# Expert rows are added to the residual in memory by an accumulating scatter, and the norm behind the first expert stage moves into the next stage

## What is computed

```python
def rms_norm(x, g):
    return x * rsqrt(mean(x * x, axis=-1) + EPS) * g
...
    h = h + hier_moe(rms_norm(h, norm2_g), ...)      # 16 experts
    return rms_norm(h[:, N_META:], final_g)          # end of the first block
...
    u = rms_norm_2(h, norm_mix_g)                    # start of the second
...
    h = h + hier_moe_2(rms_norm_2(h, norm_ffn_g), ...)   # 32 experts; this is the output
```

## Time and profile before

| | us |
|---|---|
| median of 3 runs | 3065.0 |
| lowest and highest | 3061.52, 3066.18 |
| the profiled execution | 3058.05 |
| its span | 3056.3 |
| TensorE busy | 2683.7 (88%) |
| VectorE busy | 1508.0 (49%) |
| ScalarE busy | 1099.9 (36%) |
| GpSimd busy | 861.0 (28%) |

### The profile page before, as it was taken

The page is one execution under the profiler, slowest core; times in us unless marked ns, Lnnn a source line. Parts: engine busy times, 40 slices in busy tenths (PEclk is TensorE's granted clock), DMA queues, the critical chain, the costliest instruction groups (busy, mean ns, idle before and its releaser), DMA issues. The chain is left out here.

```text
span 3056.3 us, 33957 instructions
## 1 busy us (share of the span) xinstructions
PE 2683.7 (88%) x11990; PEld 1975.7 (65%) x11990; DVE 1508.0 (49%) x1832; ACT 1099.9 (36%) x1445; POOL 861.0 (28%) x748
## 2 busy tenths in 40 slices
PE   5999898999989699909999799898999989599994
PEld 3898555777768577706655455556777868577773
DVE  4295341222223588743266545443433543588885
ACT  3012332000012377741133344441331332377773
POOL 1232421212212154422100232322333322155441
PEclk9999899999999799958999899998999999799997
DMA  3110112112123599952422222322112113499998
GB/s 92 36 49 14 41 36 58 48 34 55 34 74 134 196 365 373 358 222 56 205 62 62 73 64 75 82 63 75 41 48 55 48 71 136 175 344 348 350 334 312
DMA packets 220932, 404.99 MB, mean 133 GB/s; under 512 B 41656, under 2 KB 160776, under 8 KB 198056
## 3 DMA queue, kind: packets, MB, share of 16 engines
q1 hardware_dynamic: 203560, 370.21, 35.8%
q0 software_dynamic: 17280, 33.59, 2.9%
HBM read 351.97 MB, written 76.68 MB: 140 GB/s over the span
## 5 line engine op out<-in xcount | busy, mean ns | idle before, releaser
L1920 DVE TENSOR_TENSOR moe_run_w_low_up<-moe_run_w,moe_run_w_high_up 128x2048 fp32r<-128x2048 f32 x116 | 265.4, 2289 | 103.4 <-ACT moe_run_w_high_up L1751 102.9
L1751 ACT CAST moe_run_w_high_up<-moe_run_w 128x2048 fp32r<-128x2048 f32 x116 | 221.3, 1908 | 103.1 <-DMA moe_run_w<-w_gate 54.0
L1697 PE MATMUL moe_run_up<-moe_run_w_high_up,moe_run_xT_high 128*128 128x512 f32 x464 | 193.4, 417 | 11.0 <-issue 10.9
L134 PE MATMUL rnn_ps<-uT_again_high,rnn_w_high 128*128 128x512 f32 x512 | 201.7, 394 | 0.0
L134 PE MATMUL rnn_ps<-uT_again_low,rnn_w_high 128*128 128x512 f32 x512 | 199.7, 390 | 0.0
L134 PE MATMUL rnn_ps<-uT_again_high,rnn_w_low 128*128 128x512 f32 x512 | 199.7, 390 | 0.0
L1697 PE MATMUL moe_run_up<-moe_run_w_low_up,moe_run_xT_high 128*128 128x512 f32 x464 | 184.0, 397 | 0.0
L1697 PE MATMUL moe_run_up<-moe_run_w_high_up,moe_run_xT_low 128*128 128x512 f32 x464 | 184.0, 397 | 0.0
L1225 DVE TENSOR_TENSOR merge_gated<-merge_branch,merge_gate 128x512 f32<-128x512 f32 x48 | 33.2, 691 | 302.1 <-ACT merge_gate L1210 302.1
L134 PE MATMUL merge_gates<-uT_high,merge_wg_high 128*128 128x512 f32 x384 | 170.2, 443 | 0.0
L1071 ACT ACTIVATE mla_probs<-mla_scores 128x512 f32<-128x512 f32 x192 | 94.2, 490 | 193.2 <-PE mla_scores L1003 138.6
(11 more groups left out here) (483 smaller groups left out, 6858.5 us busy)
## 6 DMA issues: line engine op xcount, KB each, us to landing
moe_run_w<-exp_w SPq DMA_DIRECT2D x72, 1024.0 KB, 9.0
moe_run_w<-w_gate SPq DMA_DIRECT2D x34, 1024.0 KB, 9.0
moe_run_w<-w_up SPq DMA_DIRECT2D x34, 1024.0 KB, 12.0
moe_run_w<-w_down SPq DMA_DIRECT2D x34, 1024.0 KB, 6.8
rnn_raw<-w_in SPq DMA_DIRECT2D x32, 512.0 KB, 3.9
merge_raw<-w_in SPq DMA_DIRECT2D x24, 512.0 KB, 3.8
norm_x<-x SPq DMA_DIRECT2D x16, 512.0 KB, 4.7
out_h<-x SPq DMA_DIRECT2D x16, 512.0 KB, 4.5
```

The source lines that it names most:

```text
L134: last = pe.matmul(out, a, b, start=(k == 0), stop=(k == n - 1))
L1697: last = pe.matmul(up[p][:], a, w, start=(h == 0 and k == 0), stop=(h == 1 and k == 3 * HK - 1))
L1751: act.copy(hi[p][j], raw[p][j][:]).then_inc(s_hi[j], 1)
L1920: dve.tensor_tensor(lo[p][j], raw[p][j][:], hi[p][j].bitcast(F32), ALU.subtract).then_inc(s_lo[j], 1)
```

## The change

In both expert stages the scatter goes to the residual itself (`h_d`, in the second stage the output) and adds the rows to what stands there. So ScalarE multiplies a result by a column of weights, `place_w`, as it copies it out of PSUM. That column holds the weight for each slot of each block; the stage's start computes it by one-hot products on TensorE, as the row numbers are. A scatter waits until the one before it has landed. One copy of two columns of `token` serves the scatter of block b and the gather of block b + 4, since both use token rows; it is made before the result is there. The table `y_d`, the loads of h and of `y_d`, the sums and the stores behind the loop are gone.

The norm with `final_g` moves into `norm3`: this stage loads the residual, makes the first norm in place, stores it to `x2` for later use, and makes its own norm of it into another tile, `z`. Each tile is squared, rooted and scaled twice.

```diff
-def norm_to_features(nc, cst, name, load, g_row, uT, first, prefetch):
+def norm_to_features(nc, cst, name, load, g_row, uT, first, prefetch, ahead=None):
...
+            def keep(sp, t):
+                sp.wait_ge(s_norm_a, t + 1)
+                sp.dma_start(ahead[1][t * P:(t + 1) * P, :], x[t % R][:]).then_inc(s_kept[t % R], 16)
...
+                    if t == 1 and ahead:
+                        sp.dma_start(ga[:], ahead[0].to_broadcast((P, D))).then_inc(s_ga, 16)
...
-                    if t >= R:
+                    if t >= R and ahead:
+                        keep(sp, t - R)
+                        sp.wait_ge(s_norm, t - R + 1)
+                        sp.wait_ge(s_kept[t % R], 16 * (t // R))
+                    elif t >= R:
                         sp.wait_ge(s_turn, 2 * (t - R) + 2)
...
+                if ahead:
+                    for t in range(n - R, n):
+                        keep(sp, t)
+                    for r in range(R):
+                        sp.wait_ge(s_kept[r], 16 * n // R)
...
+                def first_norm(t):
+                    act.wait_ge(s_x[t % R], 16 * (t // R) + 16)
+                    if t > 1:
+                        act.wait_ge(s_sum, t - 1)
+                    act.activation(junk[:], x[t % R][:], ACT.Square, accum_out=ss_a[:, t:t + 1]).then_inc(s_sum_a, 1)
+                    act.wait_ge(s_mean_a, t + 1)
+                    act.activation(root_a[:, t:t + 1], ms_a[:, t:t + 1], ACT.Sqrt).then_inc(s_root_a, 1)
+
+                def second_squares(t):
+                    act.wait_ge(s_norm_a, t + 1)
+                    act.wait_ge(s_sum_a, min(t + 2, n))
+                    act.activation(junk[:], x[t % R][:], ACT.Square, accum_out=ss[:, t:t + 1]).then_inc(s_sum, 1)
...
+                        if ahead:
+                            first_norm(t + 1)
...
+                        if ahead:
+                            second_squares(t)
...
+                def first_norm(t):
+                    at = slice(t, t + 1)
+                    dve.wait_ge(s_sum_a, t + 1)
+                    dve.tensor_scalar(ms_a[:, at], ss_a[:, at], 1.0 / D, EPS, ALU.mult, ALU.add).then_inc(s_mean_a, 1)
+                    dve.wait_ge(s_root_a, t + 1)
+                    dve.reciprocal(inv_a[:, at], root_a[:, at]).then_inc(s_inv_a, 1)
+                    if t == 0:
+                        dve.wait_ge(s_ga, 16)
+                    dve.wait_ge(s_inv_a, t + 1)
+                    dve.scalar_tensor_tensor(out=x[t % R][:], in0=x[t % R][:], scalar=inv_a[:, at], in1=ga[:],
+                                             op0=ALU.mult, op1=ALU.mult).then_inc(s_norm_a, 1)
...
-                        dve.scalar_tensor_tensor(out=x[t % R][0:rows, :], in0=x[t % R][0:rows, :],
+                        if ahead and t >= 2:
+                            dve.wait_ge(s_turn, 2 * (t - 2) + 2)
+                        dve.scalar_tensor_tensor(out=normed(t)[0:rows, :], in0=x[t % R][0:rows, :],
                                                  scalar=inv[0:rows, at], in1=g[0:rows, :], op0=ALU.mult,
                                                  op1=ALU.mult).then_inc(s_norm, 1)
...
-def run_experts(nc, cst, name, experts, logits, w1, w3, w2, v_d, y_d, h_d, g_row, out_d):
+def run_experts(nc, cst, name, experts, logits, w1, w3, w2, v_d, h_d):
...
-                if g_row is not None:
-                    sp.dma_start(g, g_row.to_broadcast((P, D))).then_inc(s_g, 16)
-                for t in range(NT):
-                    if t % 2 == 0:
-                        sp.wait_ge(s_lo[t // 2 % 2], 2 * n + 1 + t // 4)
-                    sp.dma_start(h[t], h_d[t * P:(t + 1) * P, :]).then_inc(s_h[t], 16)
                 for p in range(2):
                     sp.wait_ge(s_st[p], 16 * n + 16)
-                for t in range(NT):
-                    for k in range(2):
-                        at0 = k * S + t * P
-                        sp.dma_start(yk[t][k], y_d[at0:at0 + P, :]).then_inc(s_yk[t], 16)
-                for t in range(NT):
-                    if g_row is not None:
-                        sp.wait_ge(s_out, t + 1)
-                    else:
-                        sp.wait_ge(s_sum, t + 1)
-                    sp.dma_start(out_d[t * P:(t + 1) * P, :], h[t]).then_inc(s_kept, 16)
-                sp.wait_ge(s_kept, 16 * NT)
+                sp.sem_inc(s_go, 1)
...
-                def gather(b, p):
-                    pool.tensor_copy(idx[p][:], token[:, bass.ds(b, 1)]).then_inc(s_idx, 1)
-                    pool.wait_ge(s_idx, b - 1)
+                def gather(p):
                     pool.sem_inc(s_go, 1)
                     pool.indirect_dma_start(
                         out=x[p][:], out_offset=None, in_=v_d,
-                        in_offset=bass.IndirectOffsetOnAxis(ap=idx[p][:, 0:1], axis=0),
+                        in_offset=bass.IndirectOffsetOnAxis(ap=rows[p][:, 1:2], axis=0),
                         bounds_check=S - 1, oob_is_err=False).then_inc(s_x[p], 16)
 
-                def scatter(i, p):
-                    b = 2 * i + p
-                    pool.wait_ge(s_y, b + 1 + Y0)
-                    pool.sem_inc(s_go, 1)
-                    pool.tensor_copy(to[p][:], choice[:, bass.ds(b, 1)]).then_inc(s_to, 1)
-                    pool.wait_ge(s_to, b + 1)
+                def scatter(i, p, first=False):
+                    pool.wait_ge(s_y, 2 * i + p + 1 + Y0)
+                    if not (first and p == 0):
+                        pool.wait_ge(s_st[1 - p], 16 * i + 16 * p)
                     pool.sem_inc(s_go, 1)
                     pool.indirect_dma_start(
-                        out=y_d, out_offset=bass.IndirectOffsetOnAxis(ap=to[p][:, 0:1], axis=0),
+                        out=h_d, out_offset=bass.IndirectOffsetOnAxis(ap=rows[p][:, 0:1], axis=0),
                         in_=y[p][:], in_offset=None,
-                        bounds_check=2 * S - 1, oob_is_err=False).then_inc(s_st[p], 16)
+                        bounds_check=S - 1, oob_is_err=False, compute_op=ALU.add).then_inc(s_st[p], 16)
...
-                    gather(2 + p, p)
+                    pool.tensor_copy(rows[p][:, 1:2], token[:, 2 + p:3 + p]).then_inc(s_rows, 1)
+                    pool.wait_ge(s_rows, p + 1)
+                    gather(p)
                 pool.wait_ge(s_list, 1)
                 n = more(pool)
-                with pool.Fori(0, n) as i:
+
+                def one_pass(i, first=False):
                     for p in range(2):
-                        b = 2 * i + p + 4
-                        pool.wait_ge(s_turn, b - 1)
+                        b = 2 * i + p
+                        pool.wait_ge(s_turn, b + 3)
                         pool.sem_inc(s_go, 1)
-                        gather(b, p)
-                        scatter(i, p)
+                        pool.tensor_copy(rows[p][:], token[:, bass.ds(b, 2, 4)]).then_inc(s_rows, 1)
+                        pool.wait_ge(s_rows, b + 3)
+                        gather(p)
+                        scatter(i, p, first)
+
+                one_pass(0, True)
+                with pool.Fori(1, n) as i:
+                    one_pass(i)
                 for p in range(2):
+                    pool.tensor_copy(rows[p][:, 0:1], token[:, bass.ds(2 * n + p, 1)]).then_inc(s_rows, 1)
+                    pool.wait_ge(s_rows, 2 * n + p + 3)
                     scatter(n, p)
                 for p in range(2):
                     pool.wait_ge(s_x[p], 16 * n + 32)
                     pool.sem_inc(s_go, 1)
-                if g_row is not None:
-                    for t in range(NT):
-                        pool.wait_ge(s_h[t], 16)
-                        pool.wait_ge(s_weighted, t + 1)
-                        pool.tensor_tensor(h[t], h[t], y[t % 2][:], ALU.add).then_inc(s_first, 1)
...
+                def place_weights(k):
+                    pe.wait_ge(s_weighted, k + 1)
+                    for t in range(NT):
+                        last = pe.matmul(ps_w[:, 0:NB], in_block[k][:, t, :].bitcast(F32), weight_of[k][:, t, :],
+                                         start=(k == 0 and t == 0), stop=(k == 1 and t == NT - 1))
+                    last.then_inc(s_wsum, 1)
+
+                place_weights(0)
                 turn_rows(0, 0, True)
+                place_weights(1)
...
-                    act.copy(y[p][:], down[:]).then_inc(s_y, 1)
+                    act.mul(y[p][:], down[:], place_w[:, bass.ds(b, 1)]).then_inc(s_y, 1)
...
+                dve.wait_ge(s_exp, 2)
+                own(dve.tensor_reduce(tmp[:], gx[:], AX.X, ALU.add))
+                own(dve.reciprocal(gw[:], tmp[:]))
+                own(TS(tmp[:], ex[:], 1.0, None, ALU.add))
+                own(dve.reciprocal(tmp[:], tmp[:]))
+                own(TT(weights[:, 0, :], gw[:], tmp[:], ALU.mult))
+                own(TT(weights[:, 1, :], weights[:, 0, :], ex[:], ALU.mult))
...
-                own(TS(choice[:], ps_id[:, 0:NB], 2.0 * S, None, ALU.add))
...
```

(26 more changed lines are left out.)

118 lines of the change are left out of this document (45 added, 73 removed).

## The result

The changed kernel takes 3030.26 us (median of 4 runs, 3029.62 to 3033.17), the kernel before took 3063.26 us beside it (3059.08 to 3066.18). The ratio is 0.9895, with a 95% interval of 0.9878 to 0.9912: 33 us, 1.05%, faster. The profiled execution took 3029.62 us, its span is 3027.9 us against 3056.3. Two later comparisons, on two different chips, gave 0.9896 (0.9875 to 0.9916) and 0.9922 (0.9903 to 0.9941).

What follows compares the result with a forecast made beforehand. Nearly full TensorE and DMA engines, paced by weights landing, bound the loops. Saved 34 + 52 = 86, paid 22 + 3 + 30 = 55, net -31 us from the 3065.0 median: 3034 us, range 3014 to 3059 (8 in 10: 3000 to 3090).

Steps and rivals of the forecast that it cites:

- The bound of the loops: Both expert loops: TensorE and DMA engines nearly full; how soon weights land sets the pace, so added bytes cost time.
- TensorE's floor: Expert loops: TensorE's own work for one block, 9.5 us, against scatter intervals of 10.15 and 10.50 us.
- The size of the read: Expert loops: scatters also read 16.8 MB of residual, 44 us of DMA time, costing 18 + 12 = 30 us.
- today's shares: Expert loops: with DMA shares unchanged at 0.96 and 0.93, blocks take 11.1 and 11.2 us, 0.95 and 0.7 more.
- The new wait: Expert loops: each scatter waits for the previous landing; some 10.2 us against an interval of 10.8, so it just fits.
- the chain rival: Expert loops: scatters run one after another at 12 us each, costing 95 us, total 3099 us; chance 0.22.
- Doubling: Scatters in the loops: adding reads two sources at half a copy's rate, so costs a second copy, 44 us.
- The end of the kernel: Behind the second expert loop: scatter starts earlier and the tail goes, end at 3022.3, saving 34 us (33 to 35).
- The end of the first stage: Behind the first expert loop: next stage starts at 1303.7 rather than 1355.54, saving 52 us (51 to 53).
- The norm stage: Norm stage takes over the first norm: 5.3 us a tile instead of 2.7, costing 22 us (16 to 34).
- the lower bound: Norm stage: cost of 16 us if all waits between the engines are hidden.
- The start: Start of each expert stage: weight operations and sixteen products, gathers 0.9 us later; 1.5 us per stage, 3 in all.

Runs made afterwards that it cites:

- The plain: The change, but second-stage scatters write without adding and wait only for the one two blocks before; sums left out: 2990.77 us, ratio 0.9809.
- the apart: Second-stage scatters write without adding or neighbour wait, each followed by an unused gather of as many bytes; sums left out: 3026.08 us, ratio 0.9921.
- half-loaded: The change with its adding scatters and waits, but the second stage's loop loads only half of each w_down: 2990.1 us, ratio 0.9811.

## Why the prediction was right

**The bound of the loops** was read rightly. The windows showed DMA engines at 93 to 96% and blocks 0.65 and 1.0 us above TensorE's floor. The plain, the apart and the half-loaded kernels show that it is bytes that set the pace: 337 us, 364 us, 327 us.

**The size of the read** was right in sum: 44 us of DMA time predicted, 48 measured; 30 us of loop predicted, 28.8 measured in the first pair of profiles. The parts were wrong. In the first stage I took the middle between today's share and 100%, 0.73 us a block; it came out below the end that I had worked out for 100%, 10.3 us or 0.45 a block (intervals of 10.65 us up to the last but one scatter), though the share rose only from 0.96 to 0.97. In the second I took 0.35 us a block; the share did not rise at all but fell to 0.92, and the block lost 0.56 to 0.8 us, the "today's shares" end of my bound or more. Two mis-sized terms cancelled, which was luck. Reading an average share of 0.93 as room of 7% was the error: that stage could not use it, and the half-loaded kernel shows 0.92 where TensorE is busy for 97%. Why that share stays near 0.92, no run here tells.

**The new wait** was said to fit just, and it does, though not as argued. Landings took 10.4 us, as forecast (10.2), and with the 0.9 us to the next issue, which I had left out, they fill the interval. The profile puts the pace down to it. My own sign for the chain rival (GpSimd waits for landings rather than for y) appeared without the rival being true. The better sign was in the same sentence: a landing of over 11 us.

**Doubling.** The Trainium skill (Collectives: The Full Stack, The bandwidth ceiling: the fold count and why AG ≠ RS ≠ AR) says of the additions in a collective that each reads two sources and so moves at half the rate of a copy. This case agrees for scatters inside one core: 48 us for 16.8 MB written, and 4.5% of the span whether the read is in the scatter or apart.

**The end of the kernel** holds one of the largest errors of a single term: 27.4 us saved instead of 34. I had the last scatter start 0.2 us after y is copied, land in 2.15 + 1.0 us and the span end 1.3 us later. In the profile it starts 2.85 us after y's end, lands in 2.7 us and the span ends 5.6 us after that. The read alone costs less than I took: 2.7 us against 2.1 for a plain scatter with nothing else running. Of the start, 0.9 us pass in the kernels without the wait as well; the other 2.0 are the wait for the scatter before; it cost as much in one later execution and 0.1 to 0.7 us in six. The 1.3 us were taken from a stage boundary whose last transfer was a store of SyncE's. Here GpSimd issues the last transfer, and its DRAIN of 7.3 us outlasts the landing. It does so with plain writes too (6.7 us, and 5.6 us from landing to end), so it is not the addition. What it waits for, no run here tells.

**The end of the first stage** saved 46.9 rather than 52 us, by the same things: the last scatter waited for one that landed at some 1312.9, 6 us after its issue, and starts 2.8 us after y's end; then 6.7 us pass to the next load, 2.7 for the landing and 4.0 behind it, where I had 2.15 + 1.0 + 1.3.

**The norm stage** cost 16.2 us, the lower bound, not 22. I laid the tile out as one chain of 5.3 us, 4.5 of work and two waits of 0.4. Its period is 4.83: VectorE's own work is 34.14 us in eight tiles, 4.27 a tile, since neighbouring operations overlap, and the two waits cost 0.27 us each in the steady part. That is some 4 us of the 6; the other 2 lie at the stage's start or end.

**The start.** Six small operations took 1.30 us (1040.12 to 1041.42). The sixteen products for the weights were mis-sized: each half of them took 3.62 and 3.46 us where I had 1.89, as for the ids' eight.

```profile
1043.07 1.42 POOL L1665 DMA_INDIRECT moe_run_x<-v,moe_run_token  x1 [18.11 <-DVEq L1957]
...
1043.43 3.62 PE L1767 MATMUL moe_run_hturn<-moe_run_weight_of_block,moe_run_xT_high 128*128 128x32 f32 x16 [2.64 <-DVE moe_run_weight_of_block L1963]
...
1047.63 1.97 PE L1723 MATMUL moe_run_turn<-all_ident,moe_run_x 128*128 128x128 f32 x8 [0.57 <-DMA moe_run_x<-v,moe_run_token]
...
1049.40 3.46 PE L1767 MATMUL moe_run_hturn<-moe_run_weight_of_block,moe_run_xT_low 128*128 128x32 f32 x16
```

The first half is hidden behind the gather all the same; the second ends at 1052.86, 0.95 us after VectorE has the first rows' low parts. The stage began 4.0 us later in this execution (ids' first product 1036.55 against 1032.59) and its first gather 4.9 us later, so the step costs 0.9 us, as predicted; but that gather then landed sooner and the first y stands only 1.5 us later. How much of that is the change is left open.

## What to carry to other kernels

An addition in memory saves a pass behind a loop and puts its read into the loop: price it as one more transfer of the same bytes, in the place where it runs. Where the DMA engines are nearly full, moving 8.4 MB from a tail into a loop gives back most, perhaps all, of what the tail saves; where a long tail of sums and a norm went away with it, as in the first stage, it paid. When a wait becomes what the profile names, take it away in one run and take bytes away in another before believing it: here the first changed nothing and the second 31 to 35 us. And take what a stage pays behind its last transfer from a stage that ends the same way: here it was 1.3 us behind a store of SyncE's and 4.0 and 5.6 us behind a scatter of GpSimd's. Last, what the loop's bound is made of is worth a look of its own: 21 of 72 loads fetched what was there already.

## What the runs showed of the hardware

- An adding scatter holds GpSimd for 1.61 us in the median against 1.02 for a plain one; without the wait between neighbours it rose to 2.06 in the second stage, and a plain one to 1.34.
- The counted bytes of the queue don't contain the addition's read (33.60 against 33.59 MB), its time does (4.5 against 2.9%). A counted rate that falls at the same DMA share is the sign of it.
- With nothing else running, the last adding scatter landed 2.7 us after its issue and the last plain one 2.1. The one before the last, with the weights' loads over, took 4.8 us (3013.89 to 3018.70).
- Behind the last scatter of a stage GpSimd's DRAIN took 5.7 us in the first expert stage and 7.3 us in the second (6.7 with plain writes). From landing to the next stage's first load 4.0 us passed and to the end of the kernel 5.6, where 1.3 us passed behind a store of SyncE's.
- Products of 128 x 32 in plain float32 appear as 16 matrix instructions for 8 products and take 3.5 us, those on rounded operands as 8 and take 1.89 us.
- A scaling of 128x1024 by a column alone took 0.75 us on VectorE, one that also multiplies by a tile 1.28.
